# Attention scores of a 4-layer float32 block: from half-array matmuls per head to full-array matmuls on zero-padded keys, with a host-made bias and low weight parts written over the raw ring

## The chip, the cores and the metric

The kernel runs on one core of one Trainium2 chip. The metric is the device time of one execution in microseconds (us). The kernel before took 3293.68 us, the median of three runs (3292.60 to 3294.15).

## The reference, cut to what matters

256 tokens of width 2048 pass through two layers of a first block and two layers of a second one, everything in float32. The parts that the change touches are the score products:

```python
# first block: sliding-window attention, 16 heads of width 64, 4 key heads
scores = jnp.einsum('bnqgrd,bnkgd->bngrqk', qb, kb) * (SWA_HEAD_DIM ** -0.5)
# second block, mixer a: 8 heads, width 128 plus a rotated part of width 64 that all heads share on the key side
q = jnp.concatenate([q[..., :A_NOPE], apply_rope(q[..., A_NOPE:], pos)], axis=-1)
k = jnp.concatenate([kv[..., :A_NOPE], jnp.broadcast_to(kr, (b, s, HA, A_ROPE))], axis=-1)
sc = jnp.einsum('bhqd,bhkd->bhqk', qb, k).astype(jnp.float32) * scale
# mixer b: 4 heads with two halves of width 64 each, so 8 score maps
sc = jnp.einsum('bhqnd,bhknd->nbhqk', qb, k).astype(f32) * scale
# mixer c: 4 heads of width 128 with a learned bias over the distance
rel = LEFT_CHUNKS * CHUNK + jnp.arange(CHUNK)[:, None] - jnp.arange(win * CHUNK)[None, :]
bias = rel_bias[:, jnp.clip(rel, -(CHUNK - 1), REL_CLIP) + (CHUNK - 1)].astype(jnp.float32)
sc = jnp.einsum('bcqhd,bckhd->bchqk', qc, kb).astype(jnp.float32) * (C_DH ** -0.5) + bias
# and the wide products around them
proj = h @ w_in;  out = y @ w_out;  x = x + jnp.square(jax.nn.relu(h @ w_up[l])) @ w_down[l]
mod = jax.nn.silu(c) @ w_mod + b_mod      # a vector times a 2048 x 6144 matrix, per layer of the first block
```

## The kernel before, in words

**Wide products.** Every weight matrix is read in groups of two 128-row chunks by up to 512 columns (512 KB). SyncE starts the loads into a ring of six slots (`raw`). ScalarE rounds a group to the high part `w_hi` (`hi`, L637), VectorE subtracts it from the raw group to get the low part `w_lo` (`lo`, L892); both live in rings of four slots. TensorE then runs 12 matmuls for each group (`multiply`, L1430 to L1432: high times high, high times low, low times high, for two chunks and two halves of the tokens). A raw slot is free again as soon as `lo` has read it (SyncE waits on `group_read`, six groups back). `hi` may run at most four groups ahead of the matmuls (`group_multiplied`). Each engine's program issues `hi` and `lo` two groups ahead of the matmul step it belongs to.

**The vector-matrix product** for `mod` is done on VectorE (`mod_product`, L927 and L929), with its weight groups in the same ring: 64 groups before everything else, then one per step in the first 24 steps of each first-block layer, fewer in the steps after, and 24 in the steps of `out0`. So in those stretches two 512 KB loads go with each step of 12 matmuls.

**Mixers beside the products.** Each engine's program is written by a generator for the wide products and one for the mixer, which take turns: a fixed share of product steps (two or three, in the smaller jobs one or two), then one slot of the mixer. In `attention`, slot s of TensorE computes the scores of group s, transposes the probabilities of group s-1 and multiplies those of group s-2 with the values; VectorE adds the mask and finds the maximum, ScalarE does the exponentials. Groups are four heads for the first 128 queries and two heads for the second 128. `prep` lists the transposes that bring queries and keys into the layout for the scores; two of its entries make a slot.

**The scores** (L1522) are float32 matmuls, each of which appears in the trace as two MATMUL and two LDWEIGHTS. Sliding window, the rotated part of mixer a, and mixer b have a contraction of 64, and use 64 rows of the array; sliding-window heads are grouped by parity, because even heads lie in partitions 0 to 63 and odd ones in 64 to 127. The other scores contract over 128.

**The bias of mixer c** comes as reversed rows (`bias_c`, a DMA from GpSimd's queue), is flipped by a matmul with a reversed identity (L1632), and VectorE adds the mask while it empties the bank (L1249).

**GpSimd** starts the small loads and does the reciprocal square roots (`rsqrt`, L578), each behind what its program has before it.

## Time and profile before

| what | value |
|---|---|
| median of three runs | 3293.68 us |
| time of the profiled execution | 3292.71 us |
| its span | 3290.4 us |
| mean granted TensorE clock | 0.971 of full |
| TensorE busy | 3009.0 us, 91% |
| VectorE busy | 1921.1 us, 58% |
| ScalarE busy | 1495.9 us, 45% |
| DMA | 608.99 MB, mean 185 GB/s |

A timeline row gives the start, the busy time and, with `xN`, the number of instructions of that group. TensorE overlaps its instructions, so the distance between the starts of two rows tells what a group costs, and the busy time of a row reaches into the next one. The shape `64*128` in a TensorE row is a weight block of 64 rows by 128 columns, `128*64` one of 128 rows by 64 columns. The time between the profiled execution's span and its own time is 2.3 us.

### The profile page before, as it was taken

The numbers are of one execution on the slowest core, as the hardware profiler recorded it, in microseconds if no ns is written. First come the engines' busy times: TensorE is split into PE (matmuls) and PEld (weight loads), VectorE is DVE, ScalarE is ACT, GpSimd is POOL, SyncE is SP. The second block draws the span as 40 slices with busy tenths as digits, with TensorE's granted clock in tenths as the row PEclk, the third lists the DMA queues.
The fourth block names the chain that finished last, engine by engine and source line by source line (L and its number), as shares of the span: only waits on it lengthen the run. The fifth ranks groups of instructions, "written<-read, shape, count | busy, mean of one in ns | idle before, by whom it ended". The sixth has DMA issues, their size and how long they took to land.

```text
span 3290.4 us, 36557 instructions
## 1 busy us (share of the span) xinstructions
PE 3009.0 (91%) x14316; PEld 2519.4 (77%) x14316; DVE 1921.1 (58%) x2430; ACT 1495.9 (45%) x2108; POOL 54.8 (2%) x59
## 2 busy tenths in 40 slices
PE   1598989799989899989999999998998999999998
PEld 1488767689777777768888888887876788888886
DVE  7887879775655444655554555444456555445544
ACT  0355344555444554454443444455453544344443
POOL 0000010000100000000000000000000000000000
PEclk9999899899999899999999999999999999999999
DMA  9886759674434454346655665554433565566554
GB/s 343 301 291 179 228 185 314 226 263 121 147 123 148 142 165 119 124 130 187 186 192 192 188 187 188 194 170 149 138 129 115 167 189 188 192 192 186 184 195 145
DMA packets 324314, 608.99 MB, mean 185 GB/s; under 512 B 19584, under 2 KB 77072, under 8 KB 323504
## 3 DMA queue, kind: packets, MB, share of 16 engines
q1 hardware_dynamic: 322336, 600.29, 57.4%
q0 software_dynamic: 1808, 6.38, 0.7%
q8 instruction: 113, 1.85, 0.2%
q14 instruction: 57, 0.47, 0.0%
HBM read 604.50 MB, written 2.10 MB: 184 GB/s over the span
## 4 chain that ended last, share of the span: by engine, by line
PE 62%; DVE 3%; ACT 2%; issue 1%; DMA 0%; DVEq 0%; POOL 0%; ACTq 0%
PE ps L1430 19%; PE ps L1432 19%; PE ps L1431 19%; PE ps L1410 2%; PE ps L1522 1%; PE ps L1451 1%; DVE w_lo L892 1%; PE ps L1536 1%; ACT w_hi L637 1%; ACT probs L772 0%; DVE x L902 0%; ACT hf L706 0%; DVE smax L1047 0%; PE ps L1632 0%; DVE probs L1042 0%
## 5 line engine op out<-in xcount | busy, mean ns | idle before, releaser
L892 DVE TENSOR_TENSOR w_lo<-raw,w_hi 128x1024 fp32r<-128x1024 f32 (+3 forms) x996 | 1159.0, 1169 | 1099.2 <-ACT w_hi L637 1097.3
L637 ACT ACTIVATE w_hi<-raw 128x1024 fp32r<-128x1024 f32 (+3 forms) x996 | 1000.1, 1011 | 1251.6 <-PE ps L1432 1176.7
L1430 PE MATMUL ps<-w_hi,hT_hi 128*128 128x512 f32 (+2 forms) x2880 | 1128.6, 392 | 46.7 <-DVE w_lo L892 41.5
L1432 PE MATMUL ps<-w_hi,hT_lo 128*128 128x512 f32 (+2 forms) x2880 | 1103.3, 383 | 0.0
L1431 PE MATMUL ps<-w_lo,hT_hi 128*128 128x512 f32 (+2 forms) x2880 | 1100.1, 382 | 0.0
L1430 PEld LDWEIGHTS ps<-w_hi,hT_hi 128*128 128x128 f32 x2880 | 553.0, 192 | 144.5 <-issue 50.8
L1432 PEld LDWEIGHTS ps<-w_hi,hT_lo 128*128 128x128 f32 x2880 | 551.1, 191 | 92.8
L1431 PEld LDWEIGHTS ps<-w_lo,hT_hi 128*128 128x128 f32 x2880 | 553.7, 192 | 89.0 <-issue 2.2
L1430 PE MATMUL ps<-w_hi,uT_hi 128*128 128x512 f32 x1024 | 399.0, 390 | 0.0
L1432 PE MATMUL ps<-w_hi,uT_lo 128*128 128x512 f32 x1024 | 398.4, 389 | 0.0
L1431 PE MATMUL ps<-w_lo,uT_hi 128*128 128x512 f32 x1024 | 398.4, 389 | 0.0
L929 DVE SCALAR_TENSOR_TENSOR acc<-raw,c_col,acc 128x512 f32<-128x512 f32 x336 | 238.5, 751 | 13.7 <-DVE acc L929 0.5
L1430 PEld LDWEIGHTS ps<-w_hi,uT_hi 128*128 128x128 f32 x1024 | 192.2, 188 | 40.7 <-DVE uT_lo L989 0.9
L1432 PEld LDWEIGHTS ps<-w_hi,uT_lo 128*128 128x128 f32 x1024 | 192.2, 188 | 39.7
L1431 PEld LDWEIGHTS ps<-w_lo,uT_hi 128*128 128x128 f32 x1024 | 192.3, 188 | 39.6
L1440 PE MATMUL ps<-cst,acc 128*128 128x1 f32 x192 | 30.1, 278 | 104.7 <-DVE acc L934 104.7
L772 ACT ACTIVATE probs<-probs,smax 128x128 f32<-128x128 f32 (+1 forms) x144 | 65.6, 456 | 119.2 <-DVE smax L1047 68.3
L1440 PEld LDWEIGHTS ps<-cst,acc 128*128 128x128 f32 x192 | 30.8, 237 | 106.1 <-DVE acc L934 74.0
L978 DVE TENSOR_TENSOR hT_lo<-hf,hT_hi 128x512 fp32r<-128x512 f32 x80 | 55.4, 692 | 74.5 <-ACT hT_hi L711 73.6
L1410 PE MATMUL ps<-cst,proj 128*128 128x128 f32 (+2 forms) x328 | 52.4, 298 | 46.2 <-DVE proj L1292 17.0
L1410 PEld LDWEIGHTS ps<-cst,proj 128*128 128x128 f32 (+2 forms) x328 | 41.8, 147 | 56.9 <-DVE proj L1292 17.5
L902 DVE TENSOR_TENSOR x<-x,ps 128x512 f32<-128x512 f32 x80 | 54.8, 685 | 44.4 <-PE ps L1432 42.9
(211 smaller groups left out, 1665.2 us busy)
## 6 DMA issues: line engine op xcount, KB each, us to landing
raw<-in_w_up SPq DMA_DIRECT2D x256, 512.0 KB, 4.0
raw<-in_w_down SPq DMA_DIRECT2D x256, 512.0 KB, 3.6
raw<-in_w_mod SPq DMA_DIRECT2D x192, 512.0 KB, 5.0
raw<-in_w_in SPq DMA_DIRECT2D x128, 456.0 KB, 3.6
raw<-in_w_in SPq DMA_DIRECT2D x112, 512.0 KB, 4.7
raw<-in_w_in SPq DMA_DIRECT2D x96, 344.0 KB, 3.7
raw<-in_w_out SPq DMA_DIRECT2D x64, 512.0 KB, 4.7
raw<-in_w_o SPq DMA_DIRECT2D x64, 512.0 KB, 3.6
```

The source lines that it names most:

```text
L637: act.activation(w_hi[:, L % SPLIT_SLOTS, 0:c, 0:w], raw[:, G % RAW_SLOTS, 0:c, 0:w], ACT.Copy).then_inc(S.hi_ready, 1)
L772: a = act.activation(e, e, ACT.Exp, bias=smax[:, r, j:j + 1], accum_out=ssum[:, r, j:j + 1])
L892: dve.tensor_tensor(w_lo[:, s, 0:c, 0:w], raw[:, group_at[L] % RAW_SLOTS, 0:c, 0:w], w_hi[:, s, 0:c, 0:w].bitcast(F32), ALU.subtract).then ...
L902: a = dve.tensor_tensor(v, v, ps[:, bank(job, i, t)], ALU.add)
L929: m = dve.scalar_tensor_tensor(out=s, in0=w, scalar=c, in1=s, op0=ALU.mult, op1=ALU.add)
L978: dve.tensor_tensor(f(dst_lo[:, 2 * b:2 * b + 2]), f(hf[:, u % 2]), f(dst_hi[:, 2 * b:2 * b + 2]).bitcast(F32), ALU.subtract).then_inc(S.l ...
L1410: mm = pe.transpose(ps[0:rows, b, j * P:(j + 1) * P], s, ident)
L1430: pe.matmul(o, a, wh, start=k0 + c == 0, stop=False)
L1431: pe.matmul(o, a, wl, start=False, stop=False)
L1432: mm = pe.matmul(o, b, wh, start=False, stop=k0 + c == job.chunks - 1)
L1440: mm = pe.matmul(ps[:, b, j:j + 1], acc[:, t % 2, 0, j * P:(j + 1) * P], K["ones"][:, 0:1], start=True, stop=True)
L1451: mm = pe.transpose(ps[:, b, a * P:(a + 1) * P], u_nat[:, i % 2, a % 2, c * P:(c + 1) * P], ident)
```

## The change

- Queries and keys of two heads share one stationary block and one moving operand. The stationary block holds the queries of two heads of width 64, one in rows 0 to 63 and one in rows 64 to 127. The keys are stored twice with zeros: once in the upper rows with zeros below, once in the lower rows with zeros above. One matmul over all 128 rows and over both copies gives the scores of both heads. This is done for the sliding window (`k1T`), for the rotated part of mixer a (`krT`) and for mixer b (`kaT2`). Scores of each group of two heads are thus one matmul of twice the columns. The grouping by parity goes.
- The zeros are written by GpSimd with memsets ahead of each layer's sliding window and mixer b, and once for `krT`. TensorE waits for them at its first score.
- Queries of mixer b are transposed two halves at a time (4 `prep` entries instead of 8, 16 fewer transposes for each layer); the rotated parts of mixer a's queries go to a packed tensor `q_rope`, its rotated key to `k_rope` with a copy, and 8 fewer transposes are made for each layer. Banks that hold padded keys are emptied by two ScalarE instructions of 64 partitions each.
- The bias of mixer c is laid out by the host; the flip matmuls go, and VectorE adds the mask in SBUF with one instruction.
- `w_lo` has the address of `raw`: `lo` writes over the raw group. The ring has eight slots instead of six, the four separate `w_lo` slots go. A slot that held a product's group is free only when its matmuls are done.

On TensorE, the first scores of mixer a (`kaT`, `qaT` the parts of width 128, `krT`, `qrT` the rotated ones), four heads by 128 queries and 128 keys, before:

```order
L1432 MATMUL ps<-w_hi,hT_lo 128x456
L1522 MATMUL ps<-kaT,qaT 128x128
L1522 MATMUL ps<-krT,qrT 128x128
L1522 MATMUL ps<-kaT,qaT 128x128
L1522 MATMUL ps<-krT,qrT 128x128
L1522 MATMUL ps<-kaT,qaT 128x128
L1522 MATMUL ps<-krT,qrT 128x128
L1522 MATMUL ps<-kaT,qaT 128x128
L1522 MATMUL ps<-krT,qrT 128x128
L1430 MATMUL ps<-w_hi,hT_hi 128x456
```

and the same place in the changed kernel:

```order
L1504 MATMUL ps<-w_hi,hT_lo 128x456
L1595 MATMUL ps<-krT,qrT 128x256
L1595 MATMUL ps<-kaT,qaT 128x128 x2
L1595 MATMUL ps<-krT,qrT 128x256
L1595 MATMUL ps<-kaT,qaT 128x128 x2
L1502 MATMUL ps<-w_hi,hT_hi 128x456
```

Eight matmuls that alternate between 128 and 64 weight rows have become six that all use 128 rows; the columns that stream are as many.

On GpSimd, the start of the first block's second layer (`stat` is the reciprocal square root, `sgw` and `sgln` small loads), before:

```order
L578 TENSOR_TENSOR stat<-stat,minus_half 128x8
L578 TENSOR_TENSOR stat<-stat,minus_half 128x2
L592 DMA sgw<-in_sg_w 128x8x128
L593 DMA sgln<-in_sg_ln_g 128x512
L594 DMA sgln<-in_sg_ln_b 128x512
L578 TENSOR_TENSOR stat<-stat,minus_half 128x2 x2
```

and in the changed kernel:

```order
L628 TENSOR_TENSOR stat<-stat,minus_half 128x8
L628 TENSOR_TENSOR stat<-stat,minus_half 128x2
L646 MEMSET k1T 64x4x256
L648 MEMSET k1T 64x4x256
L650 DMA sgw<-in_sg_w 128x8x128
L651 DMA sgln<-in_sg_ln_g 128x512
L652 DMA sgln<-in_sg_ln_b 128x512
L628 TENSOR_TENSOR stat<-stat,minus_half 128x2 x2
```

Two memsets now stand ahead of the three loads and of the layer's first reciprocal square root.

The diff, cut to its core:

```diff
-RAW_SLOTS = 6
+RAW_SLOTS = 8
...
         raw = sb("raw", [P, RAW_SLOTS, GROUP // COLS, COLS])
+        w_lo = at("w_lo", [P, RAW_SLOTS, GROUP // COLS, COLS], F32R, cursor[0] - 4 * RAW_SLOTS * GROUP)
         w_hi = sb("w_hi", [P, SPLIT_SLOTS, GROUP // COLS, COLS], F32R)
-        w_lo = sb("w_lo", [P, SPLIT_SLOTS, GROUP // COLS, COLS], F32R)
...
+        def halves(dst, h):
+
+            return [(0, HD, dst[0:HD, h:h + 2, 0]), (HD, P, dst[HD:P, h:h + 2, 1])]
...
+        def paired(m, t, hs):
+
+            return [(j, 2, m.q(hs[j])[:, t * P:(t + 1) * P], m.k(hs[j])[:, :, 0:(t + 1) * P], True, True)
+                    for j in range(0, len(hs), 2)]
...
-        mla.qk = lambda h: [(qaT[:, h], kaT[:, h]), (qrT[:, h], krT[:])]
+        def mla_scores(t, hs):
+            n = slice(t * P, (t + 1) * P)
+            out = []
+            for j in range(0, len(hs), 2):
+                out.append((j, 2, qrT[:, hs[j] // 2, n], krT[:, :, 0:(t + 1) * P], True, False))
+                out += [(j + a, 1, qaT[:, hs[j + a], n], kaT[:, hs[j + a], 0:(t + 1) * P].unsqueeze(1), False, a == 1)
+                        for a in range(2)]
+            return out
...
-        dif.prep = head_pairs(proj2, C_QB, HD, HD, 8, qaT) + head_pairs(proj2, C_KB, HD, HD, 8, kaT)
+        dif.prep = head_pairs(proj2, C_QB, P, P, 4, qaT)
+        dif.prep += [(halves(kaT2, h), [proj2[:, t, C_KB + (h + a) * P:C_KB + (h + a + 1) * P]
+                                        for a in range(2) for t in range(TOK)]) for h in range(0, 4, 2)]
...
                 if G >= RAW_SLOTS:
-                    sp.wait_ge(S.group_read, G - RAW_SLOTS + 1)
+                    before = G - RAW_SLOTS
+                    if before in multiplied_of:
+                        sp.wait_ge(S.group_multiplied, multiplied_of[before])
+                    else:
+                        sp.wait_ge(S.group_read, before + 1)
...
                 if l:
                     pool.wait_ge(S.x_ready, 4 * l)
+                pool.memset(k1T[HD:P, :, 0], 0.0).then_inc(S.swa_padded, 1)
+                pool.wait_ge(S.swa_padded, 2 * l + 1)
+                pool.memset(k1T[0:HD, :, 1], 0.0).then_inc(S.swa_padded, 1)
+                pool.wait_ge(S.swa_padded, 2 * l + 2)
...
-                dve.tensor_tensor(w_lo[:, s, 0:c, 0:w], raw[:, group_at[L] % RAW_SLOTS, 0:c, 0:w],
-                                  w_hi[:, s, 0:c, 0:w].bitcast(F32), ALU.subtract).then_inc(S.group_read, 1)
+                r = group_at[L] % RAW_SLOTS
+                dve.tensor_tensor(w_lo[:, r, 0:c, 0:w], raw[:, r, 0:c, 0:w], w_hi[:, s, 0:c, 0:w].bitcast(F32),
+                                  ALU.subtract).then_inc(S.group_read, 1)
...
-                    a = rotate(lambda a, b: proj2[:, t, C_KR + a:C_KR + b], cos, sin, 32, [v[:, 0:32] for v in tmp])
+                    kr = proj2[:, t, C_KR:C_KR + ROPE]
+                    link(rotate(lambda a, b: kr[:, a:b], cos, sin, 32, [v[:, 0:32] for v in tmp]))
+                    a = dve.tensor_copy(k_rope[:, t], repeat(kr, 2))
...
-                for half in range(2):
-                    b = dve_bank()
-                    drained(dve.tensor_tensor(bias_c[:, 2 * half:2 * half + 2], ps[:, b].rearrange("p (h k) -> p h k", h=2),
-                                              repeat(K["chunk"], 2), ALU.add))
+                dve.wait_ge(S.rows_landed, rows_value(2, l))
+                link(dve.tensor_tensor(bias_c[:], bias_c[:], repeat(K["chunk"], 4), ALU.add))
...
-                        for j, h in enumerate(hs):
-                            parts = m.qk(h)
-                            for a, (q, k) in enumerate(parts):
-                                mm = pe.matmul(ps[:, b, j * nk:(j + 1) * nk], q[:, t * P:(t + 1) * P], k[:, 0:nk],
-                                               start=a == 0, stop=a == len(parts) - 1)
+                        o = ps[:, b, 0:len(hs) * nk].rearrange("p (h k) -> p h k", k=nk)
+                        for j, w, q, k, first, last in m.scores(t, hs):
+                            mm = pe.matmul(o[:, j:j + w], q, k, start=first, stop=last)
...
-                pe.wait_ge(S.rows_landed, rows_value(2, l))
-                for half in range(2):
-                    b = dve_bank()
-                    pe.matmul(ps[:, b], K["flip"], bias_c[:, 2 * half:2 * half + 2].rearrange("p h k -> p (h k)"),
-                              start=True, stop=True).then_inc(S.dve_bank_filled, 1)
```

## Rows read from the trace of the kernel before

**Rows 1.** The page's first part: busy time, share of the span, instructions.

```profile
PE 3009.0 (91%) x14316; PEld 2519.4 (77%) x14316; DVE 1921.1 (58%) x2430; ACT 1495.9 (45%) x2108; POOL 54.8 (2%) x59
```

**Rows 2.** What TensorE waited for: total us, times, longest.

```profile
PE ps L1430 <- DVE w_lo L892: 49.7, 16, 4.1
...
PE ps L1410 <- ACT ses L776: 8.5, 11, 1.3
...
PE ps L1410 <- DVE proj L1021: 5.7, 2, 2.9
```

**Rows 3.** TensorE in order of time, mixer a: start, busy us, operation.

```profile
1234.91 0.38 PE L1522 MATMUL ps<-kaT,qaT 128*128 128x128 f32 x2
1235.23 0.49 PE L1522 MATMUL ps<-krT,qrT 64*128 64x128 f32 x2
...
1238.14 0.47 PE L1430 MATMUL ps<-w_hi,hT_hi 128*128 128x456 f32 x1
...
1254.48 0.59 PE L1522 MATMUL ps<-kaT,qaT 128*128 128x256 f32 x2
...
1256.89 0.66 PE L1410 MATMUL ps<-cst,probs 128*128 128x128 f32 x4
```

**Rows 4.** TensorE in order of time, last transposes and scores of mixer b.

```profile
1328.50 1.03 PE L1410 MATMUL ps<-cst,proj 128*64 128x128 f32 x8
1329.29 0.48 PE L1430 MATMUL ps<-w_hi,hT_hi 128*128 128x512 f32 x1
...
1331.65 0.39 PE L1431 MATMUL ps<-w_lo,hT_hi 128*128 128x512 f32 x1
1331.88 0.39 PE L1432 MATMUL ps<-w_hi,hT_lo 128*128 128x512 f32 x1
1332.20 1.16 PE L1522 MATMUL ps<-kaT,qaT 64*128 64x128 f32 x8
1333.29 0.50 PE L1430 MATMUL ps<-w_hi,hT_hi 128*128 128x512 f32 x1
...
1349.73 1.13 PE L1522 MATMUL ps<-kaT,qaT 64*128 64x256 f32 x4
1350.79 0.66 PE L1410 MATMUL ps<-cst,probs 128*128 128x128 f32 x4
```

**Rows 5.** TensorE in order of time, first scores of mixer c.

```profile
1401.00 1.05 PE L1522 MATMUL ps<-kaT,qaT 128*128 128x128 f32 x8
1401.80 0.48 PE L1430 MATMUL ps<-w_hi,hT_hi 128*128 128x512 f32 x1
```

**Rows 6.** All engines in order of time, start of the job beside mixer c.

```profile
1387.47 3.62 PE L1632 MATMUL ps<-bias_c,cst 128*128 128x512 f32 x4
...
1389.10 1.23 DVE L892 TENSOR_TENSOR w_lo<-raw,w_hi 128x1024 fp32r<-128x1024 f32 x1 [0.25 <-ACT w_hi L637]
...
1390.47 0.93 PE L1430 MATMUL ps<-w_hi,hT_hi 128*128 128x512 f32 x1
```

**Rows 7.** Busy us by engine in the flips' stretch; then clock, DMA share, GB/s.

```profile
1387.00:1391.00 4.00, 4.00 (x9) 1.89 (x8) 2.53 (x3) 3.94 (x6) 0.00 (x0) 0.50 0.00 0
```

**Rows 8.** All engines in order of time, start of the first block's second layer.

```profile
607.66 0.54 POOL L594 DMA_DIRECT2D sgln<-in_sg_ln_b  x1
...
608.37 0.72 POOL L578 TENSOR_TENSOR stat<-stat,minus_half 128x2 f32<-128x2 f32 x1 [0.17 <-DVE stat L994]
```

**Rows 9.** Groups of GpSimd by line and shape: busy, mean ns, idle before.

```profile
L599 POOL TENSOR_TENSOR klev<-glf,gq 128x512 f32<-128x512 f32 x16 | 24.6, 1540 | 215.3 <-DVE qlev L1178 215.3
```

**Rows 10.** Busy us by engine, 150 to 200 us; then clock, DMA share, GB/s.

```profile
150.00:200.00 50.00, 50.00 (x230) 41.50 (x229) 47.01 (x61) 20.99 (x24) 0.00 (x0) 1.00 1.00 362
```

**Rows 11.** DMA issues by line, 145 to 225 us: count, KB, median us to landing.

```profile
raw<-in_w_in SPq DMA_DIRECT2D x14, 512.0 KB, 5.3
```

**Rows 12.** All engines in order of time, middle of the first job (`in0`).

```profile
165.14 1.41 DVE L929 SCALAR_TENSOR_TENSOR acc<-raw,c_col,acc 128x512 f32<-128x512 f32 x2
165.19 1.07 ACT L637 ACTIVATE w_hi<-raw 128x1024 fp32r<-128x1024 f32 x1 [1.52 <-DMA raw<-in_w_in]
```

More of the change, by code:

```diff
@@ L61 @@
 REL = 320
-REL_PAD = 384
 CONST_COLS = {}
@@ L69 @@
 _at = 0
-for _name, _n in (("ident", 128), ("flip", 128), ("ones", 128), ("swa", 256), ("chunk", 256), ("tril", 128),
+for _name, _n in (("ident", 128), ("ones", 128), ("swa", 256), ("chunk", 256), ("tril", 128),
                   ("inv_freq", HALF), ("cos2", 64), ("sin2", 64)):
@@ L372, in plan @@
                     group_at.append(len(loads) - 1)
+                    multiplied_of[len(loads) - 1] = len(group_at)
                     loaded += 1
@@ L460, in build, with __init__ @@
         class Mixer:
-            def __init__(self, heads, dk, dv, scale, probs, probsT, parity=1):
-                self.heads, self.dk, self.dv, self.scale, self.probs, self.probsT = heads, dk, dv, scale, probs, probsT
-                self.groups = []
-                for t, size in ((0, 4), (1, 2)):
-                    step = size * parity
-                    self.groups += [(t, list(range(h + p, h + p + step, parity)))
-                                    for h in range(0, heads, step) for p in range(parity)]
+            def __init__(self, heads, dv, scale, probs, probsT, padded=None):
+                self.heads, self.dv, self.scale, self.probs, self.probsT, self.padded = heads, dv, scale, probs, probsT, padded
+                self.groups = [(t, list(range(h, h + size))) for t, size in ((0, 4), (1, 2)) for h in range(0, heads, size)]
             def slots(self):
@@ L481, in spread, with flat @@
             return ap.unsqueeze(2).broadcast_to([ap.shape[0], ap.shape[-1], times])
+        def flat(ap):
+            return ap.rearrange("p h n -> p (h n)")
         def head_pairs(src, col, stride, width, heads, dst):
-            return [(dst[0:width, h:h + 2].rearrange("p h n -> p (h n)"),
+            return [([(0, P, flat(dst[:, h:h + 2]))],
                      [src[:, t, col + (h + a) * stride:col + (h + a) * stride + width]
-                      for a in range(2) for t in range(TOK)], width) for h in range(0, heads, 2)]
@@ L489, in build, with own @@
-        swa = Mixer(QH, HD, HD, HD ** -0.5, probs, probsT, parity=2)
-        swa.qk = lambda h: [(q1T[h % 2 * HD:(h % 2 + 1) * HD, h // 2], k1T[h % 2 * HD:(h % 2 + 1) * HD, h // (QH // KVH)])]
+                      for a in range(2) for t in range(TOK)]) for h in range(0, heads, 2)]
+        def halves(dst, h):
+            return [(0, HD, dst[0:HD, h:h + 2, 0]), (HD, P, dst[HD:P, h:h + 2, 1])]
+        def own(m, t, hs):
+            return [(j, 1, m.q(h)[:, t * P:(t + 1) * P], m.k(h)[:, 0:(t + 1) * P].unsqueeze(1), True, True)
+                    for j, h in enumerate(hs)]
@@ L501, in build @@
+        mla.scores = mla_scores
         mla.v = lambda h, kk: kv[:, kk, h * 256 + NOPE:(h + 1) * 256]
-        mla.prep = (head_pairs(qm, 0, 192, NOPE, HA, qaT) + head_pairs(qm, NOPE, 192, ROPE, HA, qrT)
+        mla.prep = (head_pairs(qm, 0, 192, NOPE, HA, qaT)
+                    + [([(0, P, flat(qrT[:, h:h + 2]))], [q_rope[:, t, 2 * (h + a):2 * (h + a) + 2].rearrange("p h d -> p (h d)")
+                                                          for a in range(2) for t in range(TOK)]) for h in range(0, HA // 2, 2)]
@@ L517, in build @@
+        chk.q = lambda h: qaT[:, h]
+        chk.k = lambda h: kaT[:, h]
+        chk.scores = lambda t, hs: own(chk, t, hs)
         chk.v = lambda h, kk: proj2[:, kk, C_VC + h * P:C_VC + (h + 1) * P]
@@ L1421, in multiply @@
                 pe.wait_ge(S.group_read, group_at[L] + 1)
-                s = L % SPLIT_SLOTS
                 k0, cnt = job.groups[j]
                 for c in range(cnt):
-                    wh, wl = (w[:, s, c, 0:job.width] for w in (w_hi, w_lo))
+                    wh = w_hi[:, L % SPLIT_SLOTS, c, 0:job.width]
+                    wl = w_lo[:, group_at[L] % RAW_SLOTS, c, 0:job.width]
                     k = job.lhs0 + k0 + c
@@ L1505, in interleave_pe, with attention @@
                 finish(mixer)
-            def attention(m):
-                for i, (dst, sources, rows) in enumerate(m.prep):
-                    transposes(sources, rows)
+            def attention(m, l):
+                for i, (_, sources) in enumerate(m.prep):
+                    transposes(sources)
                     if i % 2 or i == len(m.prep) - 1:
@@ L1661, in _ @@
                 together(fills([q, k], lambda c, t: proj2[:, t, c * P:(c + 1) * P]), products([q, k], lead=True), count([q, k]))
-                interleave_pe(fills([r]), products([r]), count([r]), mla_steps(), 1 + mla.slots())
+                interleave_pe(fills([r]), products([r]), count([r]), mla_steps(l), 1 + mla.slots())
                 pe.wait_ge(S.act_evacuated, r.E + r.tiles)
```

95 lines of the change are left out of this document (63 added, 32 removed).

## The prediction

> **What bounds the kernel now.** I read the busy table first: TensorE is busy for 3009 of 3290 us [rows 1], so for most of the span an edit counts by what it takes off TensorE's own stream, and work on the other engines counts only where TensorE waits for it. The list of TensorE's waits says where (leaving out the first 120 us, in which VectorE does the first vector-matrix products and TensorE hardly works): 49.7 us for `w_lo` in 16 waits of up to 4.1 us, at the starts of jobs; 8.5 us in 11 waits for the exponentials of the sliding window; 5.7 us in 2 waits for the rotation of mixer a [rows 2]. Third, TensorE's timeline around the scores, for the distances between starts. Last, the windows and the DMA answer for the stretches in which two loads go with each step, because there the ring matters.
>
> **The scores: what a switch of the array's rows costs.** In mixer a, two MATMUL of 128 rows start at 1234.91 and the next pair, of 64 rows, at 1235.23; all 16 are through at 1238.14, 3.23 us [rows 3]. If the columns alone counted, it would be much less: eight MATMUL of 128 columns on the full array in mixer c take 0.80 us, 0.10 us each [rows 5], so 16 would take 1.65 us (at 0.103 us). The other 1.6 us stand at eight changes between 128 and 64 rows, 0.2 us each. With 256 columns the eight MATMUL take 2.41 us (1254.48 to 1256.89) [rows 3]; at double the columns, 0.213 us each, it would be 1.70 us, and four changes at 0.2 us give the rest.
>
> The change keeps the columns that stream and removes the changes. Mixer a, for each layer: two groups of four heads go from 3.23 to 1.70 us, four groups of two heads from 2.41 to 1.70; with two layers that is 4 x 1.53 + 8 x 0.71 = 11.8 us. TensorE has no other wait inside this mixer than that for the rotation, so I count all of it. One MATMUL will have 512 columns, a shape that float32 has here only in the flips: four take 3.62 us of busy time, about 0.9 us each [rows 6], against 0.43 us for twice 0.213. They ran right after a wait of TensorE, and the granted clock of that stretch is half of full, 1.2 GHz [rows 7], which accounts for the factor of two. If it were the shape, each of the 32 two-head groups (8 of mixer a, 24 of the other two) would cost 2 x 0.47 us more than I count: 30 us back. This is a rival below.
>
> Mixer b and the sliding window make one visit to 64 rows for each group. The last product before it starts at 1331.88, one distance of 0.23 us (1331.65 to 1331.88) would bring the next at 1332.11, and it starts at 1332.20; the visit then lasts 1.09 us to 1333.29 [rows 4]. On the full array it is 0.80 us [rows 5]. So a visit costs 0.38 us too much; as 256-column MATMULs may stream at 0.213 x 4 = 0.85 us, I take 0.33 us. With two heads: 1.06 + 0.09 us now [rows 4], 0.85 after, 0.30 us. The sliding window has 12 groups per layer (4 of four heads, 8 of two) and mixer b 6, which makes 36 in all: 24 x 0.31 = 7.4 us and 12 x 0.31 = 3.7 us. Of the 24 sliding-window groups 11 wait for the exponentials [rows 2]. There the wait grows by what the scores lose, since ScalarE's chain starts after the scores and is not shorter. So I take 13/24 of 7.4 us plus a little, 4.5 us, and of mixer b, which has hardly such waits, 3.4 us. Bounds: nothing, to 11.1 us for both.
>
> The Trainium skill, page "TensorEngine Tiling (Array Packing)", section "Performance Considerations", speaks against this edit: with a contraction of 64 or less, two row tiles are to give up to twice the speed, which zero padding gives away. The rows do not show that speed before: eight 64-row MATMULs take 1.09 us, more than eight 128-row ones (0.80 us) [rows 4, 5]. By the page the scores of 64 rows could have been cut by half; by the rows there is nothing that the padding loses.
>
> **Transposes.** Eight transposes take 0.79 us (1328.50 to 1329.29) [rows 4], 0.10 us each. Mixer b loses 16 for each layer, mixer a 8: 2 x 24 x 0.10 = 4.8 us, and three changes of data type at about 0.1 us with them: 5.2 us. They lie in slots without waits; I count all of it. ScalarE's part of it (mixer b 8 evacuations before, 6 after; the sliding window 2 more, mixer a one instruction fewer) is covered by the two product steps of the slot.
>
> **The flips.** Four MATMULs for each layer start at 1387.47 and the first product at 1390.47. But this product needs `w_lo`, whose row ends at 1390.33 [rows 6]. Without the flips TensorE would stand still until the same moment: I count 0.1 us for each layer, 0.2 us. Bounds: 0 to 2 x 3.0 us. What hides it is the chain that splits the activations and the first weights of the job; if it got shorter, the flips' time would be won too. VectorE's one addition of 1024 columns replaces two of 512: nothing.
>
> **Rotation of mixer a.** VectorE gets a link and a copy of 128 columns twice per layer, before `rotated`, for which TensorE already waits 2.85 us [rows 2]. All of it lands on TensorE. A VectorE instruction with 1024 columns takes 1.23 us [rows 6]; the copy is an eighth of it plus a fixed part, between 0.15 and 0.6 us. I take 0.25: +1.0 us over two layers.
>
> **The zeros.** No row has a memset of this size on GpSimd. Eight of the ten are covered: four at the program's start and four of mixer b, which come some 25 us before its first scores. Two are not. At the second layer of the first block GpSimd is done with its three loads at 607.66 + 0.54 = 608.20 us, and `stat`, on which the normalised activations and then TensorE wait, starts at 608.37, held up by VectorE for 0.17 us [rows 8]. Two memsets ahead of the loads delay this by their whole length. They write 1024 elements in each of 64 partitions. The nearest row is GpSimd's product of 512 elements with two inputs, 1.54 us [rows 9]: from above 3.1 us each; from below 0.3 us. A memset has no input, so I take half of the upper end, 1.5 us each: +3 us, once (0.5 to 6). The start's four delay only `sgw`, which is wanted much later.
>
> The Trainium skill, page "GPSIMD Engine Reference", section 3.1, gives 1.03 cycles for each element of an instruction with little to do; an estimate from it, at 1.2 GHz, is 0.9 us for each memset, and this term would be +1.8 us. No row here shows it.
>
> **The ring.** Before, a slot is free when VectorE has read it, and the ring is six deep beyond that point; after, a product's slot is held until its 12 matmuls are done, and the ring is eight deep from there. As up to four groups may be split ahead, what remains for loads on their way is about four slots. In the MLPs (one load for each 2.73 us, 12 x 0.2275) this is 10.9 us of lead; with loads of 5 us and a split of 2.3 us it suffices. In the first jobs it is tight: two loads for each step, DMA share 1.00, 362 GB/s, VectorE busy 47 of 50 us, while TensorE starves nowhere [rows 10]. Worked out as a loop over four steps (8 slots, 2 loads each): the end of step L frees the slot, the load lands 5.3 us later (the median, in a queue of several) [rows 11], ScalarE needs 1.07 us [rows 12], VectorE 1.23 us [rows 6]: 7.6 us, and 8.2 us (three steps) are there until the matmuls of step L+4. It holds with 0.6 us to spare, and with more since fewer loads are queued at a time. Against that VectorE, with 1.41 + 1.23 = 2.64 us of work for each 2.73 us step [rows 12, 6], can hardly catch up once it has been held up, and the mixer's VectorE work stands behind these splits. I take +3 us for such slips in the jobs of the first block, with ends at -2 us (two more groups are there when a job starts) and +44 us (rival 1). The low part written over its own input costs nothing that I can see: the instruction has the same shape.
>
> **Sum**, against the profiled execution's 3292.7 us (0.97 us under the median): -11.8 - 4.5 - 3.4 - 5.2 - 0.2 + 1.0 + 3.0 + 3.0 = -18.1 us, so 3274.6 us, and 3275.6 us as a median.
>
> **Rivals.**
> 1. *The ring starves the jobs with two loads per step.* If the load lands only after 5.8 us and VectorE has a vector-matrix instruction pair (1.41 us) ahead of the split, the loop is 5.8 + 1.07 + 1.41 + 1.23 + 2.73 = 12.2 us for four steps, 3.06 us each instead of 2.73. It decides from 10.9 us on. On the 72 steps of `in0`, `out0` and `in1` this is 24 us, and where the mixer's softmax stands behind the late split in the first layer, about 20 slots more with 1 us each: +44 instead of +3, 3317 us. For it: DMA share 1.00 and VectorE at 94% [rows 10]. Against it: the loop above has room by medians. 12%.
> 2. *Half clock or waits take the gain of the small scores.* Sliding window, mixer b and the transposes give nothing, as the softmax chain sets each slot: 3275.6 + 4.5 + 3.4 + 3 = 3286.5 us. For it: 11 waits for `ses`. Against: they are 0.8 us each. 14%.
> 3. *It does not do what it says:* a 512-column float32 MATMUL costs 0.9 us at full clock too. 30 us come back: slower, 3275.6 + 30 = 3306 us. If it is only partly so, about 3290. Against: 128 and 256 columns cost 0.10 and 0.21 us, in proportion. 5%.
> 4. *The deeper ring helps* and all scores count in full: 3275.6 - 5 - 4 = 3267 us or less. 8%.
>
> **How the numbers follow.** My forecast, with its own range of 3267 to 3285 us, has 61%. The measurement tells 0.2%, 6.6 us, from no change. Faster (below 3287.1): the forecast, rival 4, and half of rival 2: 61 + 8 + 7 = 76%. Same: half of rival 2, a part of 3, and a mild form of rival 1: 7 + 1 + 4 = 12%. Slower: the rest, 12%. The range reaches to 3262 below (all scores at their upper ends) and to 3300 above, where the mild form of rival 1 lies; outside are the strong forms of rivals 1 and 3.
>
> **What would show it.** A row of mixer a's scores of four heads that lasts 1.7 us before the next product, and of two heads 1.7 us; no 64-row shape in it. MATMULs of 512 columns at 0.43 us distance. TensorE's wait for the normalised activations at the second layer longer by 2 to 4 us, and GpSimd rows of memsets of 1 to 2 us. The wait before the first product beside mixer c where the flips stood. For rival 1: in `in0` waits of TensorE for `w_lo` in mid-job, and SyncE waiting for matmuls where DMA is not at its full share. I am wrong if TensorE's waits for `w_lo` grow by more than 10 us, or if the scores' rows have not become shorter.

## The result, and the profile after

The changed kernel takes 3300.15 us, the median of 13 runs (3298.40 to 3306.28), against 3293.8 us for the kernel before on the same chip (13 runs). The ratio is 1.0021, 95% interval 1.0012 to 1.0029: it is slower by 6.3 us. The profiled execution took 3298.99 us, with a span of 3297.2 us. I had forecast 3275.6 us, with 3262 and 3300 us as the ends of the range. So the result is 24.6 us above the forecast, just past the upper end, where I had put a mild form of rival 1 (a ring that starves the jobs).

The busy table of the changed kernel, against [rows 1]:

```profile
PE 2986.3 (91%) x14132; PEld 2505.8 (76%) x14132; DVE 1922.3 (58%) x2432; ACT 1494.9 (45%) x2106; POOL 62.5 (2%) x69
```

TensorE is busy for 22.7 us less, which is about what the shorter scores and transposes should give. The span is 6.8 us longer all the same, so some 30 us of idle time are new. The list of TensorE's waits shows half of it (total us, times, longest). The changed kernel, against [rows 2]:

```profile
PE ps L1502 <- DVE w_lo L962: 55.3, 20, 4.1
PE ps L1482 <- DVE proj L1364: 18.9, 2, 16.4
PE ps L1482 <- ACT ses L845: 12.4, 14, 1.3
PE ps L1660 <- issue: 8.6, 2, 5.4
PE ps L1608 <- DVE mod L1009: 8.5, 3, 3.7
```

and the same waits in the kernel before, as far as [rows 2] does not show them:

```profile
PE ps L1410 <- DVE proj L1292: 17.0, 2, 14.5
...
PE ps L1536 <- DVE mod L939: 7.1, 3, 3.2
...
PE ps L1588 <- issue: 6.3, 2, 3.1
```

The one long wait was there before; each kind has grown by a few us, `w_lo` the most, by 5.6 us. To find the place I used the semaphore events of the trace: the moment at which the last matmul group of each job is done gives the length of each job. A job is one wide product or a range of its columns. In layer 0 of the first block `in0`, `rest0` and `z0` are three column ranges of the input product (the mixers' matmuls lie in `rest0` and `z0`) and `out0` is the output product; `in1` to `out1` are the same for layer 1. In the second block `rest2` runs beside mixer a, `oa` beside mixer b and `ob` beside mixer c; `oc` follows. In the table, `ring 8` is the first experiment below (the kernel before with only the new ring), `scores` the one that keeps the ring and the sliding window of before. Jobs that are not listed differ by at most 1.3 us each.

```
job      before   after minus before   ring 8 minus before   scores minus before
in0      199.9          +2.0                 +2.1                  0.0
rest0    151.1          +3.4                 +8.2                 -0.1
z0       134.8          +5.7                 +8.6                 -0.1
out0     109.8          +3.1                 +3.5                  0.0
in1       92.4          +4.8                 +2.1                  0.0
rest1    144.9          +2.7                 +2.8                 -0.2
z1,out1  226.6          +2.1                 +3.1                 +3.1
rest2+oa 210.3          -9.7                 -0.1                 -9.7
ob, oc    73.7          +1.7                 -0.4                 +1.3
```

(The last two rows are of layer 0; layer 1 has -9.6 and +2.3 for `after`. In `z1,out1` most of the growth, in all three, goes with the clock: with the same 7.2 us of idle time in `z1`, the stretch at 1.2 GHz is 6.8 us long in the kernel before and 10 to 14 us in the others. `in0` varies from 199.9 to 202.0 us between kernels that have the same ring, so its 2 us say nothing. The profiled execution of `ring 8` was the slowest of its five.) The first block loses 24 us. `rest2` and `oa` of the two layers win 19.3 us, where I had forecast 12.5 and 6.9 us for mixers a and b; `ob` and `oc` lose 4.0 us.

The scores themselves did what the prediction said. TensorE in order of time, changed kernel, first four-head and first two-head group of mixer a, against [rows 3]:

```profile
1255.10 0.37 PE L1504 MATMUL ps<-w_hi,hT_lo 128*128 128x456 f32 x1
1255.31 0.59 PE L1595 MATMUL ps<-krT,qrT 128*128 128x256 f32 x2
1255.74 0.61 PE L1595 MATMUL ps<-kaT,qaT 128*128 128x128 f32 x4
1256.18 0.60 PE L1595 MATMUL ps<-krT,qrT 128*128 128x256 f32 x2
1256.62 0.61 PE L1595 MATMUL ps<-kaT,qaT 128*128 128x128 f32 x4
1256.98 0.45 PE L1502 MATMUL ps<-w_hi,hT_hi 128*128 128x456 f32 x1
...
1271.76 1.02 PE L1595 MATMUL ps<-krT,qrT 128*128 128x512 f32 x2
1272.61 1.03 PE L1595 MATMUL ps<-kaT,qaT 128*128 128x256 f32 x4
1273.48 0.60 PE L1482 MATMUL ps<-cst,probs 128*128 128x128 f32 x4
```

Four heads take 1.67 us (1255.31 to 1256.98) where they took 3.23, two heads 1.72 where they took 2.41; I had written 1.70 for both. Two MATMULs of 512 columns take 0.85 us together (1271.76 to 1272.61), 0.43 each, so rival 3 is out. Mixer b, against [rows 4]:

```profile
1347.23 1.02 PE L1595 MATMUL ps<-kaT,qaT 128*128 128x256 f32 x4
1348.10 0.60 PE L1482 MATMUL ps<-cst,probs 128*128 128x128 f32 x4
...
1360.00 1.02 PE L1595 MATMUL ps<-kaT,qaT 128*128 128x512 f32 x2
1360.86 0.60 PE L1482 MATMUL ps<-cst,probs 128*128 128x128 f32 x4
```

Four score maps 0.87 us instead of 1.09, two 0.86 instead of 1.06.

### The profile page after: what moved, and what is told of

It is laid out like the page before. It is cut to its first block, busy times and chain, and to the rows that moved or that the text cites. A ratio compares the mean times of both kernels' runs of the same rounds, so it can differ in the third digit from the quotient of the medians.

```text
span 3297.2 us, 36195 instructions
## 1 busy us (share of the span) xinstructions
PE 2986.3 (91%) x14132; PEld 2505.8 (76%) x14132; DVE 1922.3 (58%) x2432; ACT 1494.9 (45%) x2106; POOL 62.5 (2%) x69
## 4 chain that ended last, share of the span: by engine, by line
PE 61%; DVE 3%; ACT 2%; issue 1%; DMA 0%; DVEq 0%; POOL 0%; ACTq 0%
PE ps L1502 19%; PE ps L1504 19%; PE ps L1503 19%; PE ps L1482 1%; DVE w_lo L962 1%; PE ps L1523 1%; PE ps L1595 1%; ACT w_hi L697 1%; PE ps L1608 1%; ACT probs L841 0%; DVE x L972 0%; ACT hf L766 0%; DVE smax L1118 0%; DVE probs L1113 0%; ACT hf L760 0%
## 5 line engine op out<-in xcount | busy, mean ns | idle before, releaser
L1512 PEld LDWEIGHTS ps<-cst,acc 128*128 128x128 f32 x192 | 30.7, 236 | 106.7 <-DVE acc L1004 74.0
L1482 PE MATMUL ps<-cst,proj 128*128 128x128 f32 x292 | 48.5, 307 | 49.3 <-DVE proj L1364 18.9
L1482 PEld LDWEIGHTS ps<-cst,proj 128*128 128x128 f32 x292 | 39.4, 158 | 59.1 <-DVE proj L1364 19.4
```

The source lines that it names most:

```text
L1482: mm = pe.transpose(ps[0:rows, b, j * P:(j + 1) * P], s, ident)
L1512: mm = pe.matmul(ps[:, b, j:j + 1], acc[:, t % 2, 0, j * P:(j + 1) * P], K["ones"][:, 0:1], start=True, stop=True)
```

## Experiments

Every run stands beside runs of the kernel before on the same chip; "before" was 3293.5, 3294.4, 3293.8 and 3294.6 us in the four groups. Where two kernels of different groups are compared, their distances to their own "before" tell more than the two medians; I give both where they differ.

**The ring alone, 8 and 10 slots**, on the kernel before (the low part written over the raw group, the slot free only behind the matmuls):

```diff
-RAW_SLOTS = 6
+RAW_SLOTS = 8        # or 10, or 9
-        w_lo = sb("w_lo", [P, SPLIT_SLOTS, GROUP // COLS, COLS], F32R)
+        w_lo = at("w_lo", [P, RAW_SLOTS, GROUP // COLS, COLS], F32R, cursor[0] - 4 * RAW_SLOTS * GROUP)
-                    sp.wait_ge(S.group_read, G - RAW_SLOTS + 1)
+                    (group_multiplied for a product's group, as in the change)
```

> The kernel before with the ring of the change alone: eight raw slots, the low part written over the raw group, a product's slot freed by its matmuls. Theory R (the ring is what costs: loads start late, and splits, softmax and vector-matrix work stand behind them): the first block loses some 20 us and the second nothing, so 3310 to 3318 us. Theory S (the first block loses by the padded sliding window: more ScalarE copies, memsets, another order of heads): 3290 to 3298 us.

> The same with ten slots, which takes as much memory as the six raw and four low slots of the kernel before. Theory R, if it is a matter of depth: four more split groups are held and six loads remain, as before, so 3291 to 3298 us. If it is not the depth but writing over the raw group or the later release as such: as slow as with eight, 3310 us or more. Theory S: 3290 to 3298 us.

Measured: 8 slots 3314.94 us (3312.0 to 3320.1), ratio 1.0063 (1.0049 to 1.0077), +21.4 us. 10 slots 3293.91 us, ratio 0.9997 (0.9988 to 1.0005). The first theory (R) had 3310 to 3318 and 3291 to 3298 us. With ten slots, writing in place and the late release cost nothing that shows; eight slots are too few. The waits in `rest0` show the chain. SyncE's queue and ScalarE, three kernels: before, then 8 slots, then 10.

```profile
SPq L562 <- DVE w_lo L892: 76.8, 47, 5.3
...
ACT w_hi L637 <- DMA raw<-in_w_in: 3.3, 2, 1.6
```
```profile
SPq L568 <- PE ps L1439: 129.3, 49, 11.2
...
ACT w_hi L643 <- DMA raw<-in_w_in: 25.2, 14, 4.6
```
```profile
SPq L568 <- PE ps L1439: 114.4, 48, 10.3
...
ACT w_hi L643 <- DMA raw<-in_w_in: 2.9, 2, 1.8
```

SyncE now waits for matmuls, up to 11 us at a time. With 10 slots nearly every load still lands before ScalarE wants it; with 8 ScalarE stands 14 times in front of a load. In `z0` it is worse, where before there is no such wait. ScalarE in `z0` with 8 slots:

```profile
ACT w_hi L643 <- DMA raw<-in_w_in: 39.7, 16, 5.3
```

TensorE in `z0`, before and then with 8 slots:

```profile
PE ps L1588 <- issue: 3.1, 1, 3.1
...
PE ps L1588 <- DVE mod L939: 0.8, 2, 0.4
```
```profile
PE ps L1595 <- issue: 5.3, 1, 5.3
PE ps L1595 <- DVE mod L946: 5.1, 2, 4.0
```

TensorE does not wait for `w_lo` there. It waits for the mixer's operands. One such wait in order of time, with 8 slots:

```profile
391.07 1.06 ACT L643 ACTIVATE w_hi<-raw 128x1024 fp32r<-128x1024 f32 x1 [3.08 <-DMA raw<-in_w_in]
...
397.02 0.69 DVE L1185 TENSOR_TENSOR qlev<-glf,gq 128x512 f32<-128x512 f32 x1 [1.62 <-ACT glf L803]
...
397.79 1.65 POOL L605 TENSOR_TENSOR klev<-glf,gq 128x512 f32<-128x512 f32 x1 [52.47 <-DVE qlev L1185]
...
399.54 0.76 PE L1595 MATMUL ps<-qlev,klev 64*128 64x128 f32 x2 [5.32 <-issue]
```

ScalarE stands 3.08 us in front of a late load. The mixer's `glf` comes behind that split in ScalarE's program, VectorE's `qlev` and GpSimd's `klev` come behind `glf`, and TensorE starts 0.1 us after `klev` ends, at 399.44 us. The kernel before has the same wait with 3.1 us. That the other waits in these two jobs have grown in the same way is read from the order of the programs and not followed one by one. TensorE idles for 15.6 us instead of 7.9 in `z0`, and the time at 1.2 GHz grows from 23.9 to 30.7 us. VectorE is busy for 77% of `z0` before, and for 75% of `rest0`, so it isn't short of time there on the whole. In `z1` and `out1`, where no loads of the vector-matrix product share the ring, the ring of 8 costs nothing: +3.1 us in the table with it and without it.

**Nine slots, alone and in the change.**

> The kernel before with an in-place ring of 9 slots as the only edit. Alone the ring cost 21 us with 8 slots and nothing with 10. If the loss falls off steeply (a load is late only where the slot's release and the load's time exceed the steps that the ring covers): 2 to 6 us, 3296 to 3300. If it falls in proportion to the missing slots: 10 us, 3304.

> The whole change with 9 in-place slots instead of 8. The ring alone cost 21 us at 8 slots and nothing at 10. If the depth decides, 9 slots take back 8 to 15 us of the change: 3285 to 3292. If the late release (a slot that comes free only behind TensorE's reading) costs by itself, whatever the depth, 3298 or more.

Measured: alone 3296.95 us, ratio 1.0005 (0.9996 to 1.0014), +2.3 us; the whole change with nine slots (`krT` in the place of `cT_hi`, zeroed once per layer, to make room) 3284.18 us, ratio 0.9970 (0.9961 to 0.9980), 16 us under the change. I had expected 3296 to 3300 and 3285 to 3292 us. The cost by depth is 21, 2 and 0 us (the last two can't be told from nothing): most of it comes with the step from nine slots to eight, where a cost in proportion would have been 10 us at nine. ScalarE's waits for loads in `rest0` go 25.2, 9.4, 2.9 us.

**Everything but ring and sliding window** (the scores and transposes of mixers a and b and the host's bias stay). Against the change:

```diff
-RAW_SLOTS = 8
+RAW_SLOTS = 6
...
+        w_lo = sb("w_lo", [P, SPLIT_SLOTS, GROUP // COLS, COLS], F32R)
...
-        k1T = A1("k1T", [P, KVH, 2, 2 * P])
+        k1T = A1("k1T", [P, KVH, 2 * P])
```

> The changed kernel with the ring of before (six raw slots, four low slots, freed on reading) and the sliding window of before (heads by parity on 64 rows, no memsets for it); the padded rotated key lies elsewhere and is zeroed once per layer to make room. Both theories leave the second block its gain, 19 us by the job times of the changed kernel's trace less some 4 us that the jobs beside and after mixer c lost: 3274 to 3280 us. If the gain of the second block hung on the ring: above 3285 us.

Measured: 3280.22 us, ratio 0.9960 (0.9947 to 0.9972), 0.2 us above the range that I had written down. That is 20 us under the change. (`krT` lies where `cT_hi` was and is zeroed in each layer; the other kernels on the ring of before have it there too.)

**The sliding window undone**, with 8 slots and with 9 (heads by parity, keys once, no memsets):

```diff
-        swa.scores = lambda t, hs: paired(swa, t, hs)
+        swa.scores = lambda t, hs: [(j, 1, q1T[h % 2 * HD:(h % 2 + 1) * HD, h // 2, t * P:(t + 1) * P],
+                                     k1T[h % 2 * HD:(h % 2 + 1) * HD, h // (QH // KVH), 0:(t + 1) * P].unsqueeze(1), True, True)
+                                    for j, h in enumerate(hs)]
```

> The changed kernel with the sliding window as before (heads by parity on 64 rows, unpadded keys, no memsets), the ring of eight kept. Theory R: the ring's loss stays and only 2 us of memsets go, while the padded scores' gain (0.3 us for each of 24 groups, partly eaten by waits) is lost too: 3298 to 3305 us. Theory S: the loss of the first block goes, 3276 to 3282 us.

> The whole change with 9 in-place slots and the sliding window of before, against 3284.2 us with the padded sliding window. With 8 slots the padded sliding window gained nothing (3300.2 against 3299.8). If the starving ring hid its gain there, here it shows: 3286 to 3289 us without it. If its slots are set by the chain through ScalarE and VectorE, or by GpSimd's memsets, 3282 to 3285.

Measured: 3299.79 us against 3300.15 with 8 slots; 3281.34 us (3279.4 to 3286.0) against 3284.18 (3278.1 to 3288.9) with 9. So the padded sliding window wins nothing that shows, with the starving ring or without (the 2.8 us against it lie within overlapping intervals, and 3281.34 us is under the lower of the two ranges that I had written down). The first of the two kernels also prices the ring beside the changed scores: it has the ring of 8 and otherwise the edits of the version that keeps the ring of before, on the same chip, and takes 19.6 us more (3299.79 against 3280.22; the place of `krT` differs too). The one with 9 slots is as far under its kernel before as the version that keeps the ring, 13.3 us. The waits of TensorE with 9 slots (at the second layer's start, then in the whole first block), padded and then undone:

```profile
PE ps L1483 <- DVE proj L1365: 16.4, 1, 16.4
...
PE ps L1483 <- ACT ses L846: 12.6, 14, 1.3
```
```profile
PE ps L1482 <- DVE proj L1364: 14.5, 1, 14.5
...
PE ps L1482 <- ACT ses L845: 9.0, 11, 1.3
```

Of the 7.4 us by which I had expected these scores to get shorter, half comes back as waiting for the exponentials (+3.6 us), 0.6 us (2.3 us with 8 slots) as waits for the padded keys' evacuation, and 1.9 us at the start of the second layer. The last is GpSimd's memsets; the changed kernel, all engines but TensorE, against [rows 8]:

```profile
620.11 0.95 POOL L646 MEMSET k1T<- 64x1024 f32 x1 [5.49 <-DVE x L1413]
...
621.11 0.94 POOL L648 MEMSET k1T<- 64x1024 f32 x1
...
624.45 0.73 POOL L628 TENSOR_TENSOR stat<-stat,minus_half 128x2 f32<-128x2 f32 x1
625.22 3.26 DVE L1364 TENSOR_SCALAR proj<-x,stat 128x512 f32<-128x512 f32 x8 [2.71 <-POOL stat L628]
```

**The memsets put behind the reciprocal square root.**

```diff
                 rsqrt(2)
+                pool.wait_ge(S.rstd_ready, 4 * l + 1)
+                pool.memset(k1T[HD:P, :, 0], 0.0).then_inc(S.swa_padded, 1)
+                pool.wait_ge(S.swa_padded, 2 * l + 1)
+                pool.memset(k1T[0:HD, :, 1], 0.0).then_inc(S.swa_padded, 1)
+                pool.wait_ge(S.swa_padded, 2 * l + 2)
```

> The changed kernel with the two memsets of k1T issued behind the layer's three small loads and first rsqrt instead of ahead of them. If they delay the layer's start by their 1.9 us: TensorE's longest wait for the projection 14.5 instead of 16.4 us, and with what the clock gives back 3296 to 3299 us against 3300. If something else ended that wait: 3300 and the wait unchanged.

Measured: 3300.81 us, nothing won, and TensorE's wait is 16.1 us instead of 16.4. The time is the one of the second expectation, but not for its reason (something else that ended the wait); the rows of that kernel, at the first and then at the second layer's start, say why:

```profile
122.83 4.79 DVE L1365 TENSOR_SCALAR proj<-x,stat 128x512 f32<-128x512 f32 x8 [0.84 <-POOL stat L628]
...
628.83 4.79 DVE L1365 TENSOR_SCALAR proj<-x,stat 128x512 f32<-128x512 f32 x8 [0.84 <-POOL stat L628]
628.85 0.95 POOL L651 MEMSET k1T<- 64x1024 f32 x1
629.86 1.11 POOL L653 MEMSET k1T<- 64x1024 f32 x1
```

The wait for `stat` is back at 0.84 us, but the same eight VectorE instructions that took 3.26 us now take 4.79 us, beside the two memsets. The two of the eight that overlap a memset last 1.25 us each, the other six 0.47 to 0.48 us. The delay moved from GpSimd's queue into VectorE's instructions. The edit is not a clean test either: it also moves the first layer's two memsets, which were covered at the program's start, to the same place, and TensorE's wait for `proj` there grows from 2.5 to 4.1 us.

**The flips.** The kernel before with the host's bias alone, and the scores version with the flips put back:

```diff
-                pe.wait_ge(S.rows_landed, rows_value(2, l))
-                for half in range(2):
-                    b = dve_bank()
-                    pe.matmul(ps[:, b], K["flip"], bias_c[:, 2 * half:2 * half + 2].rearrange("p h k -> p (h k)"),
-                              start=True, stop=True).then_inc(S.dve_bank_filled, 1)
```

> The kernel before with the bias laid out by the host as the only edit, so the flips are gone. The prediction's step: the flips lay beside the weights' splits, nothing to -0.2 us, 3293.3 to 3293.6. Theory F: the flips filled 3 us in which TensorE otherwise idles, the split that it waits for lands no earlier, and the clock stays at its lower level longer behind the idle stretch: +1 to +4 us, 3294.5 to 3297.5, with a wait of about 3 us for w_lo ahead of the first stage's second product. If the flips were on the path, 3.4 to 6 us are gained: 3287.5 to 3290.

> The version that keeps the ring and the sliding window of before, with the flips put back as well (bias as before). Theory F: the stretches of ob and oc lose the 1.7 and 2.3 us per layer that they had gained in length, 3276 to 3279 us against 3280.2. If those stretches grew for another reason: 3280 to 3284.

Measured: without the flips 3298.62 us, ratio 1.0015 (1.0006 to 1.0024), 4.2 us slower; with them back 3273.43 us, ratio 0.9938 (0.9926 to 0.9951), 6.8 us faster than the 3280.22 us without (7.7 us by the distances to "before"; the two intervals just touch). Both are 1 to 3 us past the end of what I had expected, in the direction of the theory that the idle time keeps the clock low. An edit that removes work from TensorE makes the kernel slower. TensorE without the flips (kernel before, host's bias), against [rows 6]:

```profile
1388.09 1.97 PE L1411 MATMUL ps<-cst,proj 128*128 128x128 f32 x8 [4.16 <-DVE proj L1245]
...
1392.85 0.77 PE L1431 MATMUL ps<-w_hi,hT_hi 128*128 128x512 f32 x1 [2.79 <-DVE w_lo L895]
```

From the transposes to the first product it is 4.76 us, as before (1385.70 to 1390.47, 4.77 us). So the flips were hidden, as predicted. But the windows behind (start, length, busy us of TensorE, its loads, VectorE, ScalarE, GpSimd; then the clock, the DMA share and GB/s) differ. Before:

```profile
1388.00:1392.00 4.00, 4.00 (x9) 1.91 (x8) 3.34 (x4) 3.97 (x6) 0.00 (x0) 0.61 0.09 29
1392.00:1396.00 4.00, 4.00 (x23) 3.39 (x22) 3.93 (x5) 2.66 (x5) 0.00 (x0) 1.00 0.77 252
```

Without the flips, with all 2.4 us later:

```profile
1388.00:1392.00 4.00, 1.97 (x8) 1.57 (x8) 1.25 (x3) 2.70 (x5) 0.00 (x0) 0.50 0.00 0
1392.00:1396.00 4.00, 3.15 (x8) 2.50 (x9) 3.74 (x5) 3.43 (x4) 0.00 (x0) 0.50 0.43 133
1396.00:1400.00 4.00, 4.00 (x21) 3.38 (x20) 2.30 (x2) 1.76 (x3) 0.00 (x0) 0.88 0.81 262
```

A clock of 0.61 over 4 us is 0.9 us at full speed: with the flips TensorE comes up to 2.4 GHz at about 1391.1, 0.7 us after its first product. Without them 0.88 puts it at about 1397.0, 4.1 us after the first product. The time at the lower level in `ob0` goes from 6.8 to 10.2 us and the job is 1.5 us longer. Over `ob` and `oc` of both layers it is 10.2 us more at 1.2 GHz and 4.6 us of length. In the pair beside the scores it is again 10.2 us more at 1.2 GHz, and 4.8 us of length. VectorE's addition, which the same edit changes, shows no wait of its own: but for `w_lo` behind the transposes, TensorE's waits in `ob0` and `oc0` are the same with and without the flips.

**Work in the idle time.** If idle time costs through the clock, matmuls whose result is not used should help. The base is the version with the scores of mixers a and b and with the flips (3273.43 us):

```diff
+            def filler(count):
+                u = n.so_far(S.dve_bank_filled)
+                pe.wait_ge(S.dve_bank_drained, u - 1)
+                for _ in range(count):
+                    pe.matmul(ps[:, 4 + u % 2], K["flip"], cst[:, 0:COLS], start=True, stop=True)
...
+                filler(4)
                 pe.wait_ge(S.yd_ready, TOK * (l + 1))
```

> The version with mixers a and b and the flips (3273.4 us), with four more float32 matmuls of 512 columns (a constant by a constant, their result is never read) while TensorE waits 4.2 us for mixer b's normalised output. Theory F (idle time of TensorE is what keeps its clock low behind a job's start): they fit into the wait, and the stretch at half clock beside mixer c gets shorter by 3.4 us per layer, 1.7 us of time each: 3269 to 3272. If it was not the idle time: 3273 to 3275, or more if they outlast the wait.

> As warm, with 12 such matmuls in the wait of 14.5 us at the start of the first block's second layer, 5 in the wait of 6.4 us ahead of the second block, and 2 in the wait of 2.0 us ahead of the job behind mixer c. Theory F: half-clock stretches at these places shrink, 3262 to 3269 us. Rival: what follows each of these waits is a second wait for the first weights' split, which keeps the clock down whatever stands ahead: no further gain, 3269 to 3274.

Measured: 3272.74 us (ratio 0.9936, 0.9922 to 0.9949) and 3271.56 us (ratio 0.9932, 0.9920 to 0.9944). Against 3273.43 us the intervals overlap, and by the distances to "before" (21.0, 21.0 and 22.2 us) the first filler gives nothing and all of them 1.2 us: a gain isn't shown. The first time lies between the two ranges that I had written down, the second in the range of the rival. The clock did follow. TensorE with the first filler:

```profile
1373.57 3.16 PE L1477 MATMUL ps<-cst 128*128 128x512 f32 x7
1377.45 1.09 PE L1486 MATMUL ps<-cst,proj 128*128 128x128 f32 x8 [0.72 <-DVE proj L1312]
1378.38 1.88 PE L1708 MATMUL ps<-bias_c,cst 128*128 128x512 f32 x4
1381.76 0.47 PE L1506 MATMUL ps<-w_hi,hT_hi 128*128 128x512 f32 x1 [1.49 <-DVE w_lo L958]
```

The half-clock time in `ob0` falls from 6.8 us to 0, the flips take 1.88 us of busy time instead of 3.62, and then TensorE waits 1.49 us for the same split: the job gets only 0.6 us shorter. With all fillers, the 12 matmuls ahead of `in1` halve its time at the low clock (20.5 to 10.2 us), and the job's length doesn't move (92.2 and 92.3 us). In these two places a faster clock is worth little, because the products behind it wait for a split.

**Mixer a alone**: the scores and transposes of mixer a, everything else as in the kernel before. Against the version with mixers a and b and the flips:

```diff
-        dif.prep = head_pairs(proj2, C_QB, P, P, 4, qaT)
+        dif.prep = [([(0, HD, flat(dst[0:HD, h:h + 2]))],
+                     [proj2[:, t, col + (h + a) * HD:col + (h + a + 1) * HD] for a in range(2) for t in range(TOK)])
+                    for col, dst in ((C_QB, qaT), (C_KB, kaT)) for h in range(0, 8, 2)]
-        dif.scores = lambda t, hs: paired(dif, t, hs)
+        dif.scores = lambda t, hs: own(dif, t, hs)
```

> The kernel before with the change's scores and transposes of mixer a alone: ring, sliding window, mixer b and the flips are as before. It splits the 21 us that the version with mixer a, mixer b and the flips gained. The prediction's terms: -11.8 scores, -1.7 transposes, +1.0 rotation, 12.5 us under before, 3281 to 3283, and mixer b is worth 7 to 8. A rival: the products fill whatever the mixer leaves, and only the transposes count for each: then both mixers are worth the same per removed instruction, 3284 to 3287.

Measured: 3279.84 us, ratio 0.9959 (0.9947 to 0.9972), -13.9 us, 1.2 us under the range that I had written down. By difference mixer b with its transposes is worth 6.4 us (3279.84 to 3273.43), or 7.1 us by the distances to "before".

The best version is the change without its ring, its sliding window and its bias. It takes 3273.4 us without and 3271.6 us with the fillers, 21 and 22 us under the kernel before, 27 and 29 under the changed kernel.

## Why the prediction was wrong

| part | predicted | measured |
|---|---|---|
| mixer a: scores, its 16 transposes, rotation | -11.8 - 1.7 + 1.0 = -12.5 | -13.9 |
| mixer b: scores and its 32 transposes | -3.4 - 3.5 = -6.9 | -6.4 (-7.1 by distances) |
| sliding window with its memsets | -4.5 + 3.0 = -1.5 | 0 (8 slots), +2.8 (9 slots) |
| flips | -0.2 | +4.2 alone, +6.8 beside the scores |
| ring of 8 | +3.0 | +21.4 alone, +19.6 beside the scores |
| sum | -18.1 | +5.3 with the flips at 4.2 and 8 slots; the change itself +6.3 |

**The ring** is the step that failed, and it alone turns the sign: the term of +3.0 us measured +21.4. The prediction worked out the loop that has two loads for each step of `in0`: 7.6 us needed, 8.2 us there, "it holds". That loop used medians, with 0.6 us to spare, and had no mixer in it; late splits with the mixer's work behind them were the +3 us. `in0` did hold (+2 at most, within its own scatter), and `out0` and `in1` lost 5.6 us together, where rival 1 put 24 us on the three. The place that pays is `rest0` and `z0`, with 16.8 of the 27.4 us in that execution up to `rest1`. There fewer loads go with a step and VectorE is busy for only 75 to 77%, but the mixer's instructions stand behind the splits: one late load delays the split, then the mixer's operands, then TensorE. Rival 1 had the mechanism and named this half of it too (20 slots with 1 us each); its chance of 12% and the term of +3 were too low, its +44 too high. Why nine slots suffice in these jobs and eight don't is not worked out; a loop with the mixer's work in it was not drawn up.

The signs that I had named as proof against me would have missed it. TensorE's waits for `w_lo` grew by 5.6 us, less than the 10 us that I had set, and the scores' rows did become shorter. The loss came in other waits.

**The flips**: the cover that I named held to 0.01 us, and the edit still cost 4.2 us. The missing step is that work in the shadow of a wait brought the clock up before the products. The fillers show the link to the clock, though not that time can be won by it. Beside the scores the jobs that the flips touch differ by 4.8 us in the profiled executions, and the whole executions by 3.8; the rest of the 6.8 us between the medians is not explained and may be scatter.

**The sliding window**: I had set aside 11 of 24 groups as waiting anyway. After, 14 wait, longer, so half of the saving went into `ses`; the rest went into the second evacuation of the padded keys, which I had called covered by product steps though the first score waits for it, and into the memsets. These cost 1.9 us, predicted 3.0: each took 0.95 us where I had taken 1.5; the estimate of 0.9 us that stood beside it was nearer.

**Right**: the price of a change of rows (0.2 us), 512 columns at 0.43 us, the rotation (wait for `k_rope` 6.8 instead of 5.7 us, +1.1 for a predicted +1.0), and mixers a and b with their transposes to within 1.4 us each; the transposes were not measured by themselves. I had weighed a rule of the Trainium skill (page "TensorEngine Tiling (Array Packing)", sections "Theoretical Speedup" and "Performance Considerations"): two tiles of 64 rows give up to twice the speed, which the padding gives away. For matmuls issued one after the other the measurement decides for the padding: mixer b's four maps went from 1.09 to 0.87 us. Row tiles running at the same time were not tried, so no run here tests the rule itself.

## What to carry to other kernels

A ring's depth isn't judged by the median loop of the stage with the most loads: ask how long the slot is now held, count what stays for loads on their way, and look at the stages in which other work stands behind a split in the same program. Here the margin was 0.6 us, under a quarter of a step, and one slot made the difference between 2 and 21 us. Put such a ring into a run of its own before it goes in with other edits. A matmul that is hidden behind a wait isn't worth nothing: look at the granted clock in the windows behind it before you take it out. Where a score feeds a chain through other engines, shorten it only in mixers in which TensorE doesn't already wait for that chain.

## What the hardware showed unexpectedly

- Beside two GpSimd memsets of 64x1024 (0.95 and 1.11 us) eight VectorE instructions on 512 columns took 4.79 instead of 3.26 us, at the start of both layers. The two that overlap a memset took 1.25 us each, the others at most 0.48.
- Removing 3 us of hidden matmuls left TensorE at 1.2 GHz for 3.4 us longer in `ob0`, in the part where products ran; adding 3.2 us of them (in the version with the scores) took the low level away altogether in that job, which got 0.6 us shorter.
